# Moving the split weight rings of a float32r kernel from 64 to 112 bytes behind the rows, modulo 256

## The reference, cut to what matters

```python
def swiglu(h, w13, w2):
    g, u = jnp.split(h @ w13, 2, axis=-1)
    return (jax.nn.silu(g) * u) @ w2
...
        x = x + y
        x = x + swiglu(rmsnorm(x, norm_ffn_g[i]), f_w13[i], f_w2[i])
```

## Time and profile before

| | |
|---|---|
| runs | 1777.78 us median of 3 (1775.98 to 1778.49) |
| profiled execution | 1759.64 us, of which the span from first to last instruction is 1757.8 us |
| matmuls | 13,776, of which 12,528 are of the three-way kind |
| TensorE | 97% busy, granted clock 0.988 of 2.4 GHz in the mean |
| VectorE, ScalarE | 70% and 55% busy |
| DMA | 290 MB, 165 GB/s in the mean |

### The profile page before, as it was taken

One profiled execution on the slowest core, in us unless ns is written; L12 is line 12 of the kernel. 1 busy time (PEld: TensorE's weight loads), 2 busy tenths in 40 slices (PEclk: granted clock), 3 DMA queues, 4 the chain that ended last, 5 costly groups with the idle time before them and its releaser, 6 DMA issues.

```text
span 1757.8 us, 37337 instructions
## 1 busy us (share of the span) xinstructions
PE 1698.9 (97%) x13776; PEld 1605.3 (91%) x13776; DVE 1227.2 (70%) x2013; ACT 970.2 (55%) x1352; POOL 12.8 (1%) x20
## 2 busy tenths in 40 slices
PE   7999999998999999999999999999999999999997
PEld 7999999888999987569999999999999877799997
DVE  6887766586776587888776688776566665577764
ACT  4468744365775444207774445775454644468742
POOL 0000200000000000000000000000000000000000
PEclk9999999999999999999999999999999999999998
DMA  6567664533867554105666455667464431256662
GB/s 201 169 196 246 194 222 140 165 109 97 250 199 224 166 160 143 60 1 170 201 200 215 153 173 178 206 191 243 150 191 132 142 134 61 72 162 198 194 224 71
DMA packets 79545, 290.15 MB, mean 165 GB/s; under 512 B 9739, under 2 KB 12140, under 8 KB 79340
## 3 DMA queue, kind: packets, MB, share of 16 engines
q1 hardware_dynamic: 79468, 289.11, 52.6%
HBM read 288.03 MB, written 1.05 MB: 164 GB/s over the span
## 4 chain that ended last, share of the span: by engine, by line
PE 82%; DVE 12%; ACT 2%; issue 2%; DVEq 1%; DMA 0%; SPq 0%; ACTq 0%
PE bank L570 24%; PE bank L572 23%; PE bank L571 23%; DVE wlo L1516 3%; PE bank L858 2%; PE bank L845 1%; DVE rinv L1522 1%; DVE conv_cv L1625 1%; PE bank L799 1%; PE bank L954 1%; ACT whi L1148 1%; PE bank L1050 1%; DVE hy_z L1765 1%; PE bank L1023 1%; PE bank L1060 1%
## 5 line engine op out<-in xcount | busy, mean ns | idle before, releaser
L1148 ACT CAST whi<-raw 128x1024 fp32r<-128x1024 f32 (+1 forms) x490 | 538.5, 1100 | 332.8 <-PE bank L572 290.6
L570 PE MATMUL bank<-xq_h,whi 128*128 128x256 f32 x2384 | 667.1, 280 | 8.7 <-DVE wlo L1516 8.6
L572 PE MATMUL bank<-xq_h,wlo 128*128 128x256 f32 x2384 | 660.5, 277 | 0.0
L571 PE MATMUL bank<-xq_l,whi 128*128 128x256 f32 x2384 | 660.5, 277 | 0.0
L1516 DVE TENSOR_TENSOR wlo<-raw,whi 128x1024 fp32r<-128x1024 f32 (+1 forms) x491 | 629.1, 1281 | 5.3 <-ACT whi L1148 2.7
L570 PEld LDWEIGHTS bank<-xq_h,whi 128*128 128x128 f32 x2384 | 448.0, 188 | 19.8 <-DVE wlo L1516 13.1
L571 PEld LDWEIGHTS bank<-xq_l,whi 128*128 128x128 f32 x2384 | 448.2, 188 | 1.5 <-issue 1.5
L572 PEld LDWEIGHTS bank<-xq_h,wlo 128*128 128x128 f32 x2384 | 448.6, 188 | 0.0
L570 PE MATMUL bank<-ffn_hh,whi 128*128 128x256 f32 x880 | 242.9, 276 | 0.0
L571 PE MATMUL bank<-ffn_hl,whi 128*128 128x256 f32 x880 | 242.9, 276 | 0.0
L572 PE MATMUL bank<-ffn_hh,wlo 128*128 128x256 f32 x880 | 242.9, 276 | 0.0
(11 more groups left out here) (336 smaller groups left out, 2375.6 us busy)
## 6 DMA issues: line engine op xcount, KB each, us to landing
raw<-in_w SPq DMA_DIRECT2D x414, 512.0 KB, 3.6
raw<-in_w SPq DMA_DIRECT2D x80, 704.0 KB, 4.2
att_bias<-in_bias SPq DMA_DIRECT2D x4, 512.0 KB, 6.0
hy_w<-in_filt_w SPq DMA_DIRECT2D x8, 256.0 KB, 5.0
hy_decay<-in_decay SPq DMA_DIRECT2D x4, 512.0 KB, 4.3
mla_uq<-in_uq SPq DMA_DIRECT2D x1, 1152.0 KB, 5.2
x<-in_xT SPq DMA_DIRECT2D x1, 1024.0 KB, 5.9
out<-x SPq DMA_DIRECT2D x8, 128.0 KB, 2.0
```

The source lines that it names most:

```text
L570: pe.matmul(ps, whi[:, slot, wc], hi[:, k, cols], start=first, stop=False)
L571: pe.matmul(ps, whi[:, slot, wc], lo[:, k, cols], start=False, stop=False)
L572: mm = pe.matmul(ps, wlo[:, slot, wc], hi[:, k, cols], start=False, stop=last)
L1148: nc.scalar.copy(slices(whi, p % RING, k, to), raw_slices(p % RING, k, to)).then_inc(panel_hi, 1)
```

## The change

It changes addresses alone. No instruction is added, taken away or moved in order, on any engine. `whi` and `wlo` get 12 floats (48 bytes, `W_AT`) ahead of their first slot, and 48 floats of filler stand between them, so that both start at 128 + 48 = 176 modulo 256. The tiles behind them (`x`, `xq_h`, `xh` and so on) move up by 320 bytes; `XROW_AT` goes from 48 to 32 floats and `align_rows` from 32 to 16, which keeps all rows of 256 tokens at 64 modulo 256. The rows `xh` and `xl` move by 64 bytes modulo 256, and `L_FIRST` grows by 16 floats (64 bytes) to follow. All weights then stand 112 bytes behind their rows modulo 256; in the wide panels the first load of a slice stands 112 + 64 = 176 behind the rows being read. `raw` stays where it was, a multiple of 64 bytes; `whi` and `wlo` now start at 48 modulo 64.

```diff
-XROW_AT = 48
+W_AT = 12
+XROW_AT = 32
...
-L_FIRST = {SEQ: 2 * META, L: META}
+L_FIRST = {SEQ: 3 * META, L: 2 * META}
...
-    whi = sb("whi", [P, RING, SLOT], F32R)
-    wlo = sb("wlo", [P, RING, SLOT], F32R)
+    def weight_ring(name):
+
+        flat = sb(name, [P, W_AT + RING * SLOT], F32R)
+        return flat[:, W_AT:].rearrange("p (r s) -> p r s", r=RING)
+
+    whi = weight_ring("whi")
+    sb("align_weights", [P, 48])
+    wlo = weight_ring("wlo")
...
-    sb("align_rows", [P, 32])
+    sb("align_rows", [P, 16])
```

## The result

The change makes the kernel slower: 1811.91 us, the median of 4 runs (1809.36 to 1812.97), against 1776.88 us for the kernel before, the median of 4 runs (1755.64 to 1778.49). The ratio on record is 1.0275, with a 95% interval from 1.0223 to 1.0327; it isn't the quotient of the two medians, which is 1.020, nor of the means, which is 1.022. The loss is clear of noise; its size, with three of the four runs of before near 1777 us and one at 1756, is less so. The profiled execution of after took 1812.31 us, its span 1810.5 us.

A forecast was written before the change was run, and what follows sets the result against it. TensorE, busy 97% of the span, bounds the kernel; removing slow-pace matmuls sums to 15.0 us, less 2 us at waits, 13 us: 1777.8 - 13 = 1764.8, point 1763. The forecast's own range is 1745 to 1771; the 8-in-10 range reaches 1800.

The forecast's parts named there:

- the edge argument: All three-way matmuls: two lasting paces at 64 bytes make it look like an edge; one step away only one pace should remain.
- The prediction's own last sentence: What would make it wrong: a conflict depending on distance in steps finer than the 64 bytes this trace can show.
- The row that spoke for the right answer: Wide panels: L572 at 128 bytes lasts 281 ns, neighbours at 64 last 277 and 278; not counted fully.
- Rival 2: `up` and `down` stages: 112 acts like 128, fast pace gone, about 9,200 matmuls x 4.5 ns = 41 us, 1819 us; 18%.
- the other engines at no cost: VectorE's and ScalarE's new addresses, at 48 modulo 64, were put at nothing; VectorE has 25% room.
- The count: Three-way matmuls in the whole kernel: 12,528, unchanged by the edit.
- The 18 us between the profiled execution and the median: Median of runs over profiled execution: fixed overhead (giving 1764.8 us) or about 4000 more slow matmuls; it leaned to overhead.
- The other reading: The 18 us are more slow-pace stretches, which the change takes as well: 1777.8 - 31 = 1747 us.
- Rival 4's floor: All three-way matmuls: 4 ns of the fast 113.3 are an ever-present conflict; 48 us more gained, about 1716 us; 3%.
- The rule: Skill text: TensorE has two independent read ports and never waits on anyone, so distance can't matter and the gain is 0.

The follow-up runs named there:

- the stream: Kernel of its own with only three-way matmuls from SBUF, weights' distance varied: at 256 columns 113.33 or 117.78 ns a matmul at 64 bytes, 119.97 at 112.
- the entry: Bare matmul kernel at distances 64 and 208, entered after 0 to 252 columns of another matmul: 113.33 or 117.78 ns at 64, 116.67 at 208.
- more entries: Bare matmul kernel, rows at 64 modulo 256, distances 8, 52, 64, 76, 88, 148, 22 entries each: 76 always 113.33 ns, 8 115.56, 148 116.67, others two paces.

## Why the prediction was wrong

**The step that failed** is the edge argument, under "What speaks for and against 112 bytes": "so 64 looks like an edge, and one step away from an edge the slow pace, or the fast one, should be the only one". From it I took the fast one. Two paces at one distance are no sign of a place between good and bad. They are two patterns into which the stream falls, and the entry after a wait settles which; 208, 148 and 8 bytes showed one pace alone and a slow one in 22 entries each, 76 one fast one, 52, 64 and 88 have two [the entry, more entries]. There is no edge: 60 and 68 are both worse than 64. The prediction's own last sentence names what happened: a hold that depends on the distance in steps finer than 64 bytes.

**The row that spoke for the right answer** was the earlier trace rows, 281 ns at 128 bytes beside 277 and 278. I discounted it because the wide panels never settle. The stream at 128 has 118.6 to 120.1 ns, so the row was right.

**Rival 2** ("Every load is held up", 1819 us) was right in kind: the fast pace is gone from the `up` and `down` stages. Two terms of it were mis-sized:
- its pace was taken from before's slow one, 117.8 ns, but 112 has 120.0. A matmul that was fast costs 6.7 ns more, not 4.5. The loss at the pace is 66.6 us, not 41: some 62 us of it, by 9,200 x 6.7 ns, from the matmuls that were fast, the rest from those that were slow already.
- it took nothing back, and 7.4 us of waits went; another 8.0 us (5.6 and 2.4) seem to go with the higher granted clock of that execution.

The spans of the profiled executions lie 52.7 us apart, the medians 35.0, since the profiled execution of before was one of its quicker ones, as the next point but one explains. By chance the rival's 1819 is near the 1811.9 measured.

**"It moves no instruction", and the other engines at no cost** were right. VectorE's busy time went from 1227.2 to 1229.5 us, and with 64 bytes in the otherwise changed kernel nothing is left of the loss. ScalarE's casts into `whi` took 538.5 us before and 537.2 after, VectorE's subtractions into `wlo` 629.1 and 630.1, so 48 modulo 64 costs them nothing that shows.

**The count.** The groups that the prediction names give 4136 slices or 12,408 matmuls, not 12,528; with 56 slices of smaller groups the trace has 12,576. At 4.5 ns each that moves the sum by under 1 us.

**The 18 us between the profiled execution and the median** I leaned to taking as overhead. They are the draw, as far as traces reach (none of the three runs at 1776 to 1778 us has one). The kernel before ran from 1750.3 to 1778.5 us, and in its profiled executions and those of the edits, excess and span go together (10.2 us and 1749.9; 14.4 and 1757.8; 21.1 and 1762.0; 32.8 and 1774.4). 76 bytes, with one pattern, spreads over 6.3 us in 12 runs, 8 bytes over 7.7 in 12, the kernel before over 22.6 in 19 and 25.1 in 23. The other reading, that a kernel rid of the slow pace ends near 1747, was the better one: at 76 bytes it ends at 1753.7, where the kernel before beside it had 1767.93.

**Rival 4's floor.** With a load for each matmul the stream never went under 111.6 ns, at 128 to 224 columns and either distance, and no distance had less than 113.3 at 256. Nothing of the 4 ns and the 48 us of that rival was found.

**The rule.** The Trainium skill, "SBUF — State Buffer", section "Who interferes with whom", gives TensorE two independent read ports and says that it never waits on anyone. The second holds against other engines as far as these runs show: the stream, with the others idle, has the same 113.3, 117.8 and 120.0 ns as the kernel. The independence doesn't hold here: with nothing else at work the pace follows the distance between the weights that are loaded and the rows that are read.

**What stays open.** Which addresses of a load and of a row meet, and so why 52, 64, 76 and 88 are good, wasn't found. Weights lay 512 and rows 1024 bytes apart in every run outside the wide panels, so whether the period is 256 or 512 bytes can't be told. Placement at an equal distance moves 112 by 1 to 3 ns, and 76 had 120.0 in one stretch with rows at 0. The wide panels, whose distance changes with each slice, have 116.4 ns with 256 columns in the mean at 88 bytes and 117.4 to 118.9 at the other settings tried; distances of their own weren't tried. Which of the two reads is held, and what in an entry settles the pattern, is open as well.

## What to carry to other kernels

Where TensorE loads new weights for each float32r matmul of 256 columns, measure the distance between weights and rows in steps of 4 bytes in a bare stream, with the rows placed as in the kernel and some twenty entries each, and choose one whose pace is the lowest in all of them; neither a round number nor a neighbour of a good distance says anything. Two paces of one instruction in a trace, at one clock and without waits, meant two patterns here, and a spread of 25 us between runs came with them. A gain at the pace can be worth less than its sum where other engines are waited for in between, and a loss too (here 7 of 67 us). Before a longer step is called a wait, look whether the engine stood idle ahead of it, and at the granted clock around it.

## What the runs showed of the hardware that was not expected

- Three-way float32r matmuls of 256 columns take 113.3 to 122.2 ns each at 2.4 GHz (most often 113.33, 116.67, 117.78, 118.33 or 120.00), depending on how many bytes the weights stand behind the rows, in steps as fine as 4 bytes. The paces looked at step by step are short exact patterns (600 ns in five, 1060 in nine, 340 in three).
- At one distance two patterns can be stable, and one is settled at each entry after a wait, for hundreds of matmuls (64 bytes: 113.33 ns in 22 of 44 stretches, 117.78 in the others).
- Up to 224 columns the pace is 111.7 ns and neither of the two distances tried makes a difference; 288 columns take 132.2 to 133.3 ns, 320 146.7, 384 173.3 to 177.8, 512 233.3.
- One load in three at 112 bytes, the others at 64, costs four fifths of what all three at 112 cost (118.7 and 120.0 ns against 113.3), and all kinds of matmul pay alike (282 ns each).
